# First LayerNorm of a hybrid decoder step: weight and bias on ScalarE, the first up and gate tiles taken chunk by chunk

## The reference

```
h = layer_norm(ALPHA * x + mix, ln1_w, ln1_b)          # over 1024 features, per row
u = h @ w_up ; g = h @ w_gate                          # 1024 x 2816 each
acc = conv_b + sum_i up[:, i:i+t] * conv_w[i]          # 3 taps along the sequence
a = gelu(acc) * g
y = layer_norm(ALPHA * h + a @ w_down, ln2_w, ln2_b)

def layer_norm(x, w, b):
    mu = mean(x) ; var = mean((x - mu)**2)
    return (x - mu) * rsqrt(var + 1e-5) * w + b
```

## Time and profile before

| | |
|---|---|
| median of 3 runs | 2155.69 us (2155.26 to 2162.72) |
| the profiled execution | 2155.08 us, its span 2153.4 |
| mean granted TensorE clock | 0.966 |
| TensorE busy | 92% of the span |
| VectorE / ScalarE / GpSimd busy | 54% / 30% / 10% |

### The profile page before, as it was taken

The page is one execution under the profiler, slowest core; times in us unless marked ns, Lnnn a source line. Parts: engine busy times, 40 slices in busy tenths (PEclk is TensorE's granted clock), DMA queues, the critical chain, the costliest instruction groups (busy, mean ns, idle before and its releaser), DMA issues.

```text
span 2153.4 us, 39105 instructions
## 1 busy us (share of the span) xinstructions
PE 1989.2 (92%) x14335; PEld 1861.6 (86%) x14335; DVE 1158.9 (54%) x1771; ACT 648.8 (30%) x1179; POOL 217.0 (10%) x253
## 2 busy tenths in 40 slices
PE   7998998899899999979898899799999999999996
PEld 5896887888798888768798897799999999999996
DVE  4654554968857866875423856633322333233348
ACT  4444444134134123313411003443301322123224
POOL 1000000020020020010000100400000000100004
PEclk9999999999999999989999999899999999999999
DMA  4211102697977878777822310111111111111154
GB/s 128 60 40 41 40 21 86 215 321 251 320 248 241 308 262 272 263 276 238 288 89 88 110 49 20 35 44 49 49 49 40 49 46 44 46 49 42 46 144 130
DMA packets 151681, 276.50 MB, mean 128 GB/s; under 512 B 19041, under 2 KB 57950, under 8 KB 151542
## 3 DMA queue, kind: packets, MB, share of 16 engines
q1 hardware_dynamic: 115970, 175.26, 24.2%
q0 software_dynamic: 23232, 82.80, 13.0%
q10 hardware_dynamic: 12368, 16.88, 2.1%
HBM read 247.24 MB, written 27.72 MB: 128 GB/s over the span
## 4 chain that ended last, share of the span: by engine, by line
PE 43%; DVE 5%; DMA 1%; issue 1%; ACT 1%; DVEq 0%; SPq 0%; ACTq 0%
PE bank L121 39%; PE bank L1661 3%; DVE x_lo L1889 1%; DMA gated_raw<-gated_t_scratch 1%; DVE chunk_tmp L1818 1%; DVE chunk_tmp L1820 0%; DVE z L1886 0%; DVE moving_lo L1824 0%; PE banks L1619 0%; DVE merged_hi L1822 0%; DVE w_lo L1959 0%; DMA tail_raw<-in_w_down_dram 0%; DVE y L1935 0%; DMA z<-fox_t_scratch 0%; PE banks L1647 0%
## 5 line engine op out<-in xcount | busy, mean ns | idle before, releaser
L121 PE MATMUL bank<-x_hi,w_hi 128*128 128x344 f32 (+1 forms) x1944 | 642.4, 330 | 41.1 <-DVE x_lo L1889 15.8
L121 PE MATMUL bank<-x_lo,w_hi 128*128 128x344 f32 (+1 forms) x1944 | 632.1, 325 | 0.0
L121 PE MATMUL bank<-x_hi,w_lo 128*128 128x344 f32 (+1 forms) x1944 | 631.5, 325 | 0.0
L121 PEld LDWEIGHTS bank<-x_hi,w_hi 128*128 128x128 f32 (+1 forms) x1944 | 373.2, 192 | 58.4 <-issue 46.0
L121 PEld LDWEIGHTS bank<-x_lo,w_hi 128*128 128x128 f32 (+1 forms) x1944 | 373.0, 192 | 1.6
L121 PEld LDWEIGHTS bank<-x_hi,w_lo 128*128 128x128 f32 (+1 forms) x1944 | 372.7, 192 | 1.7
L97 ACT ACTIVATE w_hi<-w_raw 128x1024 fp32r<-128x1024 f32 (+3 forms) x139 | 142.1, 1022 | 458.8 <-PE bank L121 424.5
L121 PE MATMUL bank<-moving_hi,w_hi 128*128 128x344 f32 x744 | 227.1, 327 | 13.7 <-DVE moving_hi L1797 7.0
L121 PE MATMUL bank<-moving_lo,w_hi 128*128 128x344 f32 x744 | 237.5, 319 | 0.0
L104 DVE TENSOR_TENSOR w_lo<-w_raw,w_hi 128x1024 fp32r<-128x1024 f32 (+3 forms) x139 | 164.7, 1185 | 132.5 <-ACT w_hi L97 130.6
L121 PE MATMUL bank<-moving_hi,w_lo 128*128 128x344 f32 x648 | 208.3, 321 | 0.0
(11 more groups left out here) (275 smaller groups left out, 2776.5 us busy)
## 6 DMA issues: line engine op xcount, KB each, us to landing
cache_keys<-in_cache_k_dram SPq DMA_DIRECT2D x256, 256.0 KB, 4.7
cache_vals<-in_cache_v_dram SPq DMA_DIRECT2D x256, 256.0 KB, 5.2
w_raw<-in_w_in_dram POOLq DMA_DIRECT2D x52, 512.0 KB, 6.2
w_raw<-in_w_up_dram POOLq DMA_DIRECT2D x22, 512.0 KB, 4.5
w_raw<-in_w_gate_dram POOLq DMA_DIRECT2D x22, 512.0 KB, 4.5
tail_raw<-in_w_down_dram SPq DMA_DIRECT2D x22, 448.0 KB, 3.8
gate<-gate_t_scratch SPq DMA_DIRECT2D x15, 516.0 KB, 3.5
w_raw<-in_w_down_dram POOLq DMA_DIRECT2D x10, 448.0 KB, 4.4
```

The source lines that it names most:

```text
L121: mm = pe.matmul(g.bank[n][0:m, 0:TC], w[slot][:, k, 0:m], x[:, k, chunk(n)], start=(k == 0 and i == 0), stop=(k == kt - 1 and i == 2))
```

## The change

In the first norm VectorE's tile operation at L1886 becomes a plain multiplication by the reciprocal. ScalarE then applies weight and bias in one operation that writes the full h into z, and copies that to x_hi; VectorE's second operation is a plain subtraction z - x_hi. VectorE makes the first chunk's multiplications, and from there on takes turns: x_lo of a tile of chunk n, then the multiplication of the same tile of chunk n + 1. GpSimd now waits for a chunk's full h and for its eight x_lo, and multiplies by ALPHA alone. The split of the first gate weights moves ahead: on ScalarE behind the first chunk's squares, on VectorE between the first and the second centring.

TensorE takes the first feed-forward tile in another order: up of chunk 0, gate of chunk 0 (into banks 4, 5 and 7, so that up's banks need not be free), then chunk 1, then chunk 2, and it waits for each x_lo tile alone. The first tile is written out ahead of the loop on TensorE, ScalarE and VectorE; the loop starts at the second.

```
 for k in range(NCH):
-    pool.wait_ge(normed, (k + 1) * KD)
+    pool.wait_ge(h_full, (k + 1) * KD)
+    pool.wait_ge(h_lo, (k + 1) * KD)
     for t in range(KD):
-        ins = pool.tensor_scalar(acc[:, t, chunk(k)], z[:, t, chunk(k)], ln_cols[:, 1, t:t + 1], ALPHA, ALU.add, ALU.mult)
+        ins = pool.tensor_scalar(acc[:, t, chunk(k)], z[:, t, chunk(k)], ALPHA, None, ALU.mult)
     ins.then_inc(h_scaled, 1)
...
+pe.wait_ge(centred, NCH)
+pe.wait_ge(root, 2)
+for n in range(NCH):
+    for (j, slot), dst in ((up_job, bank[n]), (gate_job, gate_bank[n])):
+        pe.wait_ge(g.w_split, RING + j + 1)
+        pe.wait_ge(g.bank_free[n], ju + 1)
+        for k in range(KD):
+            pe.wait_ge(h_lo, n * KD + k + 1)
+            for q, (w, x) in enumerate(((g.w_hi, g.xh), (g.w_hi, g.xl), (g.w_lo, g.xh))):
+                mm = pe.matmul(dst[:, 0:TC], w[slot][:, k, :], x[:, k, chunk(n)], ...)
+        mm.then_inc(g.mm_chunk, 1)
+pe.wait_ge(z_part, 2)
+pe.wait_ge(g.bank_free[NCH - 1], ju + 2)
+pe.transpose(bank[3][0:NS + 2, 0:P], up[:, SEQ:SEQ + NS + 2], g.ident[:]).then_inc(cr_t, 1)
 for f0, n, ju, jd in sections:
-    with pe.Fori(0, n) as i:
-        product(g, pe, job(i * 2 + ju, ju % 2, 0), g.xh, g.xl, before=lambda k: pe.wait_ge(h_lo, (k + 1) * KD))
+    with pe.Fori(0 if f0 else 1, n) as i:
+        product(g, pe, job(i * 2 + ju, ju % 2, 0), g.xh, g.xl)
...
 def h_high(n):
     for k in range(KD):
         act.wait_ge(normed, n * KD + k + 1)
-        act.activation(g.xh[:, k, chunk(n)], z[:, k, chunk(n)], ACT.Identity, bias=ln_cols[:, 1, k:k + 1]).then_inc(h_hi, 1)
+        act.activation(z[:, k, chunk(n)], z[:, k, chunk(n)], ACT.Identity, scale=ln_cols[:, 0, k:k + 1], bias=ln_cols[:, 1, k:k + 1]).then_inc(h_full, 1)
+        act.wait_ge(h_full, n * KD + k + 1)
+        act.activation(g.xh[:, k, chunk(n)], z[:, k, chunk(n)], ACT.Copy).then_inc(h_hi, 1)
 squares(0)
+split_hi(g, act, job(JF, JF % 2, 1))
 squares(1, range(0, 3))
...
-for n in range(NCH):
-    centre(n)
+centre(0)
+split_lo(g, dve, job(JF, JF % 2, 1))
+centre(1)
+centre(2)
...
+invert(0)
+for k in range(KD):
+    scale(0, k)
+for n in range(NCH):
+    if n < NCH - 1:
+        invert(n + 1)
     for k in range(KD):
-        dve.scalar_tensor_tensor(z[:, k, chunk(n)], z[:, k, chunk(n)], ln_cols[:, 0, k:k + 1], rstd[:, chunk(n)], ALU.mult, ALU.mult).then_inc(normed, 1)
+        h_low(n, k)
+        if n < NCH - 1:
+            scale(n + 1, k)
```

More of the change, by code:

```diff
@@ L1496, in finish @@
             sem(n) for n in ("z_part", "z_done", "z_summed", "mean", "centred", "squared", "var", "root", "inv_root"))
-        normed, h_hi, h_lo, h_scaled = (sem(n) for n in ("z_normed", "h_hi", "h_lo", "h_scaled"))
+        normed, h_full, h_hi, h_lo, h_scaled = (sem(n) for n in ("z_normed", "h_full", "h_hi", "h_lo", "h_scaled"))
+        gate_bank = (g.bank[4], g.bank[5], g.bank[7])
         fc_done, c1, conv, gelu, a_hi, a_lo = (sem(n) for n in ("fc_done", "conv_first", "conv_step", "gelu", "a_hi", "a_lo"))
@@ L1723, in _, with tile @@
                 h_high(2)
-                act.wait_ge(h_lo, NCH * KD)
                 act.wait_ge(z_part, 2)
                 for s, (f0, n, ju, jd) in enumerate(sections):
-                    with act.Fori(0, n) as i:
+                    def tile(i, first):
                         f = i + f0
-                        split_hi(g, act, job(i * 2 + ju, ju % 2, 1))
+                        if not first:
+                            split_hi(g, act, job(i * 2 + ju, ju % 2, 1))
                         act.wait_ge(conv, f * 5)
@@ L1740, in _ @@
                         act.activation(act_in[:, 0:SEQ], up[:, 0:SEQ], ACT.Identity, scale=fc[:, 16:17], bias=fc[:, 19:20]).then_inc(c1, 1)
+                        if first:
+                            act.wait_ge(g.mm_chunk, NCH * (RING + ju) + 2 * NCH - 1)
                         split_hi(g, act, job(i * 2 + ju, ju % 2, 2))
@@ L1751, in _ @@
                         act.activation(cr, bank[3][0:NS + 2, 0:P], ACT.Copy).then_inc(cr_out, 1)
+                    if s == 0:
+                        tile(0, True)
+                    with act.Fori(1 if s == 0 else 0, n) as i:
+                        tile(i, False)
                     def down(it):
@@ L1883, in _, with scale, h_low, tile @@
                     dve.wait_ge(inv, n + 1)
-                    for k in range(KD):
-                        dve.scalar_tensor_tensor(z[:, k, chunk(n)], z[:, k, chunk(n)], ln_cols[:, 0, k:k + 1], rstd[:, chunk(n)], ALU.mult, ALU.mult).then_inc(normed, 1)
[L1887 to L1891, removed]
+                def scale(n, k):
+                    dve.tensor_tensor(z[:, k, chunk(n)], z[:, k, chunk(n)], rstd[:, chunk(n)], ALU.mult).then_inc(normed, 1)
+                def h_low(n, k):
+                    dve.wait_ge(h_hi, n * KD + k + 1)
+                    dve.tensor_tensor(g.xl[:, k, chunk(n)], z[:, k, chunk(n)], g.xh[:, k, chunk(n)].bitcast(F32), ALU.subtract).then_inc(h_lo, 1)
+                invert(0)
[4 more added lines that the diff above has]
+                        invert(n + 1)
+                    for k in range(KD):
+                        h_low(n, k)
+                        if n < NCH - 1:
+                            scale(n + 1, k)
                 for s, (f0, n, ju, jd) in enumerate(sections):
-                    with dve.Fori(0, n) as i:
+                    def tile(i, first):
                         f = i + f0
-                        split_lo(g, dve, job(i * 2 + ju, ju % 2, 1))
+                        if not first:
+                            split_lo(g, dve, job(i * 2 + ju, ju % 2, 1))
                         dve.wait_ge(a_lo, f)
@@ L1911, in _ @@
                         for k in range(NCH):
-                            chunk_ready(g, dve, i * 2 + ju + 1, k)
-                            dve.tensor_tensor(act_in[:, chunk(k)], act_in[:, chunk(k)], bank[k][:, 0:TC], ALU.mult).then_inc(g.bank_free[k], 1)
+                            if first:
+                                dve.wait_ge(g.mm_chunk, NCH * (RING + ju) + 2 * k + 2)
+                            else:
+                                chunk_ready(g, dve, i * 2 + ju + 1, k)
+                            dve.tensor_tensor(act_in[:, chunk(k)], act_in[:, chunk(k)], (gate_bank if first else bank)[k][:, 0:TC], ALU.mult).then_inc(g.bank_free[k], 1)
                         dve.wait_ge(a_hi, f + 1)
@@ L1916, in _ @@
                                           gh[:, ds(i, 1), :].rearrange("p a t -> p (a t)").bitcast(F32), ALU.subtract).then_inc(a_lo, 1)
+                    if s == 0:
+                        tile(0, True)
+                    with dve.Fori(1 if s == 0 else 0, n) as i:
+                        tile(i, False)
                     def down(it):
```

12 lines of the change are left out of this document (10 added, 2 removed).

## The result

| | before | after |
|---|---|---|
| median of 20 runs each | 2159.25 us | 2162.49 us |
| ratio of the two | | 1.0018 (1.001 to 1.0026) |
| profiled execution, its span | 2155.08, 2153.4 | 2158.70, 2156.4 |
| mean granted clock | 0.966 | 0.973 |

The change makes the kernel slower by 0.18%, 3.9 us by the ratio (2.2 to 5.6). The ratio compares undisturbed executions alone (one of the 20 before took 2266.63 us) and is not the quotient of the two medians. The forecast was 2158.0 against the 2155.69 of the runs then at hand, 2.3 us slower; set on the later median of before it would be 2161.6.

The account below looks back on a forecast made before the run. TensorE, busy 92% of the span, bounds the kernel, so only its waits or lower clock count. Tile 1's start +0.5 and clock +2.2 make +2.7 on 2155.08; with 0.6 to the median, 2158 us, range 2151 to 2165.

Parts of the forecast that it names:

- Rival A: Between tile 0 and tile 1: the late weight load takes the late norm's place; +1 to +7 us, chance 0.50.
- 1. The split between the centrings: First norm: VectorE's weight split waits for ScalarE's, making the weight-and-bias step start 3.9 us late.
- 2. ScalarE's pair: Weight-and-bias step: Identity, then a Copy waiting for it, 1.22 us a tile (bounds 1.10 and 1.30) over 24 tiles.
- 3. VectorE's operations: Norm: two plain operations a tile at 0.50 us each, less than ScalarE's 1.22, so ScalarE paces.
- 4. TensorE's end of tile 0: TensorE ends the first feed-forward tile at 1381.4 to 1383.6 us, 7 to 9 us before 1390.6.
- 5. The third scaling: GpSimd's queue: third scaling starts at last x_lo, takes 5.3 us (4.3 to 6.9); tile 1's load issued at 1382.4.
- rivals B and D: First: change works as drawn, about 2152 us, chance 0.20. Second: nothing to see, within 1.5 us of before, 0.15.
- 6. From the landing to tile 1: Weights landed to tile 1: ScalarE's split, table load, gelu and VectorE's gate product, 4.1 us; tile 1 starts +0.5.
- 7. The clock: Tile 1: after idling some 8 us TensorE runs at the lower clock, costing 2.2 us (bounds 1.8 and 2.6).
- Rival B: ScalarE's pair and GpSimd's queue: the change works as drawn and time falls to about 2152 us; chance 0.20.
- Rival C: Norm's variance sums: TensorE falls to the lower clock and paces ScalarE's squares; +7 to +11 us, chance 0.15.
- The port rule: GpSimd's remaining third scalings wait behind VectorE's two 1.28 us convolution operations, 1.6 us more for the whole.

Follow-up runs that it names:

- e4: The changed kernel with tile 1's two weight loads issued ahead of GpSimd's 24 scaling operations instead of behind them; ratio to before 0.996.
- e3: The changed kernel with VectorE's split of the gate weights behind the third centring instead of the first; ratio to before 1.001.
- e2: The changed kernel with GpSimd's scaling as two operations with two constants (times ALPHA, plus 0.0); ratio to before 0.9999.
- e8: The changed kernel's order with the arithmetic of before, tile 1's loads ahead of the scaling, VectorE's weight split behind the third centring; ratio to before 0.9953.
- e5: The changed kernel's order with the norm's arithmetic of before; ratio to before 0.9989.
- e9: e7 with up's evictions alone freeing banks 0 to 2 and tile 1's weight split ahead of the taps; ratio to before 0.9938.
- e7: The changed kernel with the edits of e2, e3 and e4 together; ratio to before 0.9951.

## Why the prediction came out as it did

**Right in sign and place.** Rival A, the forecast, is what happened: TensorE waits between tile 0 and tile 1 for the gate product, behind gelu and the late weights, and pays the lower clock. e4 shows it by moving the loads alone. The time was inside the range, and the size (+2.7 forecast, +4.9 in the trace to tile 2, 3.9 by the ratio) is near, in part by luck (5. below). The wait itself was 15.3 us, about twice the 7 to 10 that I had named as a sign.

Part by part:
1. The split between the centrings: 3.9 worked out; 2.9 in the comparison with before (14.3 to 17.3), 3.5 by taking it away (e3). The 0.6 between the two are the longer variance sums of before; 3.5 is the like-for-like figure.
2. ScalarE's pair: 1.22 worked out, 1.09 measured, just under my lower bound of 1.10. The wait of 0.24 that I took from L1740 is 0.04 here, while the Identity takes 0.66 instead of 0.58. The bound was also loose as written: the bounds of its one varied term, 0.34 and 0.44, give 1.16 and 1.26, not 1.10 and 1.30. Over 24 tiles the pair's miss is 3.1 us; with step 1's 0.9 E was at 44.5 instead of 48.5.
3. VectorE's operations: 0.43 apart instead of 0.50; it did not matter, as ScalarE paced.
4. TensorE's end of tile 0: at 49.4, 3.4 us before the early end of my forecast, following E.
5. The third scaling: here the step failed in size. I put eight operations at 5.3 us, with the price of the old form, and did not ask whether one operation fewer is a cheaper or a dearer form. It is twice as dear, 1.03 us, as e2 shows by the operation alone. The third scaling was then not bound by E at all but by the second, and the load left 1.9 us later than I had it, not 4.0 earlier as E alone would give. Two misses of 4 us and 6 us, of opposite sign, left the sum near the truth. Had GpSimd kept its old price, the change would have come out at nothing or a little faster (e2: tile 2 1.2 us earlier than before), on the side of rivals B and D, and my forecast would have been wrong.
6. From the landing to tile 1: 4.1 worked out, 4.0 from ScalarE's start at 1388.54; the landing took 4.9 from the issue, not 4.7, so the gate load right behind it cost 0.2 at most.
7. The clock: 2.2 and 2.3. It did not follow the length of the idle: tile 1 was longer than 22.66 us by 1.8 after an idle of 2.6 us (e8), by 1.6 after 3.3 (e4), by 2.7 after 5.3 (e5) and by 2.3 after 15.3.

Rival B named its threshold as E plus the scaling at 1379.7, 51.1 from the first square; they came to 55.7. Rival C, the lower clock in the variance sums after the split, did not come: after idles of 1.95 and 1.00 us the sums ran at 1.00. What it described is seen on a smaller scale in the first eight sums, after the idle of 2.67 us that the kernel before has too. The port rule of the Trainium skill ("SBUF — State Buffer", "Who interferes with whom") would have made step 5 6.9 instead of 5.3, by the prediction. The trace agrees that there is blocking, and makes it small here: the operations of the third scaling follow each other at 1.03 us but for the two beside VectorE's taps, at 1.41 and 1.67 (1376.39, 1377.80, 1379.47), 1.0 us in all. It is larger in e5, where one scaling operation took 4.24 us beside VectorE's eight subtractions.

## What to carry to other kernels

When a wait is added in front of an engine's operations, look at what else stands behind them in its queue, weight loads above all; here two loads put ahead of 24 operations were worth 12.7 us in the trace, more than the other edits from the changed kernel to e9 together (8.6). Price an operation in the form in which it will be issued: dropping half of a fused operation is not always cheaper. An improvement behind another wait shows nothing: the single-tile waits were worth 0 us in the changed kernel and some 3.4 in the one without the gap. And before a difference of one or two us between two traces is put down to an edit, compare a stretch that the edit does not touch: here the first variance sums alone moved by 1.2 us.

## What the hardware showed that I had not expected

- GpSimd's tensor_scalar on 128x344 f32 with one operation (times a constant) repeats every 1.03 us; with two operations it repeats every 0.53, whether both operands are constants (4.21 us for eight, e2) or one is a column (0.53, before). One operation with a column was not run.
- A ScalarE operation that waits for the one ahead of it on the same engine started 0.04 us after its end in the norm, where one in the feed-forward part started 0.16 to 0.24 after.
- The granted clock stayed at 1.00 in tile 0 with TensorE busy for 26.46 of 29.00 us in bursts of three matmuls, and was at 0.50 for 4.5 us behind the idle of 15.3 us; after 3.3 us of idleness in e4 tile 1 still cost 1.6 us more.
- The same eight variance sums, behind the same idle of 2.67 us, took 6.58 us at a mean granted clock of 0.73 in e7 and 7.79 at 0.62 in e8.
